# Router logits from the raw residual, rstd applied afterwards; ScalarE scales and shifts; token positions in five matmuls

## What is computed

```python
h = modulate(rmsnorm(x, norm_ffn[i]), mod[:, 3], mod[:, 4])      # h * (1 + scale) + shift
x = x + mod[:, None, 5] * moe(h, w_router, b_router, wg, wu, wd)
# moe: scores = sigmoid(h @ w_router); sel = scores + b_router
# best group of 4 experts by its two largest sel, then the top 2 inside it, weights normalised
# y = sum over the chosen experts of w_e * (silu(h @ wg_e) * (h @ wu_e)) @ wd_e
```

## Time and profile before

| | us |
|---|---|
| timed executions, median of 3 | 1325.93 (1322.24 to 1326.89) |
| span of the profiled execution | 1334.2 |
| PE busy in it | 1216.7 (91%) |
| VectorE busy | 383.0 (29%) |
| ScalarE busy | 316.9 (24%) |
| GpSimd busy | 122.9 (9%) |
| mean granted TensorE clock, of full speed | 0.956 |
| mean DMA rate | 292 GB/s |

### The profile page before, as it was taken

How to read it: one execution, slowest core, us unless ns; L and a number is a source line. 1 busy time by engine, 2 the same in 40 slices (tenths; PEclk the granted TensorE clock), 3 DMA queues, 4 the chain that set the end, 5 groups by cost and what they waited for, 6 DMA issues and landing times.

```text
span 1334.2 us, 24788 instructions
## 1 busy us (share of the span) xinstructions
PE 1216.7 (91%) x10404; PEld 720.1 (54%) x10404; DVE 383.0 (29%) x1218; ACT 316.9 (24%) x716; POOL 122.9 (9%) x188
## 2 busy tenths in 40 slices
PE   4889998889998899999979999999999987799996
PEld 2446544447885554655547643445465545575553
DVE  1345111340004422611131122341541115551113
ACT  1240111331124523211133211320311114401113
POOL 2000100210000000111120000000011120001101
PEclk9898998899999999899989999999999998889998
DMA  9999999894227874799978214882769987539993
GB/s 350 415 421 420 373 409 422 287 350 169 99 95 273 293 285 180 277 382 397 407 268 322 94 70 148 348 323 94 277 262 415 414 338 301 232 139 411 389 395 136
DMA packets 89708, 389.57 MB, mean 292 GB/s; under 512 B 10456, under 2 KB 38604, under 8 KB 53240
## 3 DMA queue, kind: packets, MB, share of 16 engines
q1 hardware_dynamic: 71568, 336.61, 65.0%
q0 software_dynamic: 17456, 51.07, 10.4%
q10 hardware_dynamic: 568, 0.23, 0.1%
HBM read 370.96 MB, written 27.96 MB: 299 GB/s over the span
## 4 chain that ended last, share of the span: by engine, by line
PE 76%; DMA 11%; DVE 5%; issue 3%; ACT 2%; POOL 1%; SPq 1%; ACTq 0%; POOLq 0%; DVEq 0%
PE bank L479 70%; DMA sb_ring<-in_w_ada 3%; PE bank L954 2%; DMA sb_ring<-in_w_exp_down 2%; DMA slot_out<-sb_arena,sb_homes 2%; DMA sb_arena<-slot_out,sb_slots 2%; DVE sb_xT L1982 1%; DMA sb_arena<-in_b_ada 1%; POOL sb_arena L2120 1%; PE bank L972 1%; DMA sb_arena<-token_rows,sb_rows 1%; DMA slot_out<-sb_arena 1%; PE bank L882 0%; DVE sb_arena L1942 0%; SPq L437 0%
## 5 line engine op out<-in xcount | busy, mean ns | idle before, releaser
L479 PE MATMUL bank<-sb_ring,sb_arena 128*32 128x256 f32 (+1 forms) x6112 | 461.8, 432 | 20.6 <-DMA sb_ring<-in_w_exp_down 7.3
L479 PEld LDWEIGHTS bank<-sb_ring,sb_arena 128*32 128x32 f32 x6112 | 232.7, 112 | 192.5 <-issue 119.7
L479 PE MATMUL bank<-sb_arena 128*128 128x128 f32 (+11 forms) x776 | 141.5, 362 | 9.3 <-DVE sb_arena L1828 5.4
L479 PE MATMUL bank<-sb_ring,sb_hT 128*128 128x256 f32 x624 | 141.4, 389 | 6.2 <-ACT sb_hT L1213 6.2
L479 PEld LDWEIGHTS bank<-sb_ring,sb_hT 128*128 128x128 f32 x624 | 121.0, 195 | 27.1 <-issue 9.1
L479 PEld LDWEIGHTS bank<-sb_arena 128*128 128x128 f32 (+2 forms) x776 | 103.6, 195 | 46.1 <-issue 13.3
L479 PE MATMUL bank<-sb_ring,sb_cond 128*2 128x512 f32 x768 | 96.8, 626 | 8.1 <-DMA sb_ring<-in_w_ada 7.7
L479 PE MATMUL bank<-sb_arena,sb_ring 128*128 128x384 f32 (+2 forms) x288 | 95.5, 507 | 3.0 <-DVE sb_arena L1698 2.1
L1929 DVE TENSOR_TENSOR sb_arena<-sb_arena,bank 128x256 f32<-128x256 f32 x40 | 16.9, 421 | 263.4 <-PE bank L479 263.4
L479 PE MATMUL bank<-sb_hT,sb_ring 128*128 128x384 f32 x256 | 84.7, 493 | 2.6 <-ACT sb_hT L1213 2.6
L479 PEld LDWEIGHTS bank<-sb_arena,sb_ring 128*128 128x128 f32 (+1 forms) x288 | 49.9, 181 | 44.9 <-issue 19.0
(11 more groups left out here) (318 smaller groups left out, 1017.8 us busy)
## 6 DMA issues: line engine op xcount, KB each, us to landing
sb_ring<-in_w_ada SPq DMA_DIRECT2D x96, 1024.0 KB, 8.3
sb_ring<-in_w_exp_gate SPq DMA_DIRECT2D x60, 1024.0 KB, 17.6
sb_ring<-in_w_exp_up SPq DMA_DIRECT2D x60, 1024.0 KB, 10.6
sb_ring<-in_w_exp_down SPq DMA_DIRECT2D x60, 1024.0 KB, 16.3
sb_ring<-in_w_mlstm_in SPq DMA_DIRECT2D x12, 1024.0 KB, 16.8
token_rows<-sb_arena POOLq DMA_DIRECT2D x12, 512.0 KB, 7.4
slot_out<-sb_arena POOLq DMA_DIRECT2D x9, 512.0 KB, 8.6
sb_scratch<-in_w_exp_gate SPq DMA_DIRECT2D x4, 1024.0 KB
```

What stands on the lines that cost most here:

```text
L479: return pe.matmul(out, lhsT, rhs, start=first, stop=last)
```

## The change

- **Logits from the residual.** VectorE multiplies `w_rt` by the two amplitude columns of the layer (`router_weights`), which gives 32 stationary columns `w_ra`: 16 for context, 16 for latent tokens. PE multiplies them with the raw residual `xT`, interleaved with the squares of the norm (`raw_logits`, `norm_routed`, bank `ps[5]`). VectorE multiplies the result by `rstd`. In layer 0 the eight raw matmuls follow the last w_ada columns instead.
- **Shift.** The product of the shift vectors with `w_rt` is computed per layer in 16 one-column matmuls (`shift_logits`): in front of the output projection in layer 1, at the start of the mixer in layers 2 and 3, behind the mixer in layer 0. Three matmuls of one row add it to the folded logits, now in `ps[4]`.
- **Normalised activations.** VectorE writes `xT * rstd` in eight instructions of 384 columns. ScalarE applies amplitude and shift in one instruction for each chunk and token kind (`modulate`), the first three chunks before the exponential of the logits, five after it.
- **Order.** The fold stands before rows 0 to 3 of the w_ada group. The transposes take the first half of the channels of all tiles first (`TURNS`). Positions take five matmuls over wider ranges. Rows 4 and 5 of the w_ada group move behind the positions, next to row 6.
- Some semaphores are merged (`turns_full`, `gate_tok`), and the arena is 96 columns smaller.

```diff
+TURNS = [0, 2, 4, 1, 3, 5]
...
+        w_ra = sb("w_ra", [P, KC, 2, NE])
...
-            def norm(n):
-                for k in range(KC):
+            def norm_squares(n, a, b):
+                for k in range(a, b):
                     if k % 2 == 0 or k == KC - 1:
                         pe.wait_ge(sq_ready, 6 * n + (k // 2 + 1 if k < KC - 1 else 5))
                     q = k % 4
                     ins = mm(ps[6][32 * q:32 * q + 32, 0:TOK], mean_ones[:, 0:32], sq[:, k, :], k < 4, k >= 4)
-                ins.then_inc(ms_full, 1)
+                if b == KC:
+                    ins.then_inc(ms_full, 1)
+
+            def norm_mean(n):
                 pe.wait_ge(sq_ready, 6 * n + 6)
                 mm(ps[6][:, 0:TOK], mean_ones[:, 32:32 + P], rstd[:, :], True, True).then_inc(ms_full, 1)
+
+            def norm(n):
+                norm_squares(n, 0, KC)
+                norm_mean(n)
+
+            def raw_logits(L, n, a, b):
+                pe.wait_ge(wra_ready, L + 1)
+                for k in range(a, b):
+                    pe.wait_ge(x_ready, 8 * n + k + 1)
+                    q = k % 4
+                    ins = mm(ps[5][32 * q:32 * q + 32, 0:TOK], w_ra[:, k, :, :].rearrange("p c e -> p (c e)"), xT[:, k, :],
+                             k < 4, k >= 4)
+                    if k >= 4:
+                        ins.then_inc(lg_full, 1)
+
+            def shift_logits(L, bank):
+                pe.wait_ge(mod_added, 3 * L + 2)
+                for c in range(2):
+                    for k in range(KC):
+                        ins = mm(bank[0:1, c * NE:(c + 1) * NE], mod[:, L, 24 + k, c:c + 1], w_rt[:, k, :], k == 0, k == KC - 1)
+                ins.then_inc(sr_full, 1)
+
+            def norm_routed(L, n):
+                if L == 0:
+                    norm(n)
+                    ada(2, 6, 7)
+                    ada_columns(2)
+                    raw_logits(L, n, 0, KC)
+                else:
+                    for a, b in ((0, 2), (2, 4), (4, 6), (6, 7), (7, 8)):
+                        raw_logits(L, n, a, b)
+                        norm_squares(n, a, b)
+                    norm_mean(n)
+                pe.wait_ge(sr_ready, L + 1)
+                for t in range(NT):
+                    c = min(t, 1)
+                    mm(ps[4][:, t * NE:(t + 1) * NE], ones[0:1, :], shift_row[:, c * NE:(c + 1) * NE], t == 0, False)
+                pe.wait_ge(lg_ready, L + 1 + (L > 0))
+                for t in range(NT):
+                    c = min(t, 1)
+                    ins = mm(ps[4][:, t * NE:(t + 1) * NE], lg[:, t * P:(t + 1) * P], fold[:, c * NE:(c + 1) * NE], False, t == NT - 1)
+                ins.then_inc(rt_full, 1)
...
+                if r:
+                    shift_logits(3, ps[7])
...
+                shift_logits(1, ps[5])
 
                 project(r, lambda k: (qT if k % 2 == 0 else kT)[:, k // 2, :], hsT_ready, [8] * KC)
...
+                shift_logits(2, ps[7])
...
             def experts(L, n):
-                side(ps[6], w_rt, n)
-                for c in range(2 * NT):
-                    if c == 2:
-                        unfold(ps[6], L + 1 + (L > 0), rt_full)
+                for c in TURNS:
+                    pe.wait_ge(h_ready, 16 * n + (8 if c % 2 == 0 else 16))
+                    if c == 4:
+                        pe.wait_ge(rt_e, L + 1)
                     for k in range(4):
                         ins = pe.transpose(ps[c][:, k * P:(k + 1) * P],
                                            hT[:, 4 * (c % 2) + k, (c // 2) * P:(c // 2 + 1) * P], ident[:, :])
                     ins.then_inc(ht_full, 1)
 
-                for g in ADA_WINDOW[L]:
-                    ada(g, 4, 5)
                 pe.wait_ge(mask_ready, L + 1)
                 pick = rt[:, 5, :]
-                for t in range(NT + 1):
-                    for q in range(min(t, NT - 1) + 1):
-                        ins = mm(ps[6][:, 64 + t * NE:64 + (t + 1) * NE], tri[:, 0:P] if q == t else ones[:, :],
-                                 pick[:, q * NE:(q + 1) * NE], q == 0, q == min(t, NT - 1))
-                ins.then_inc(pos_full, 1)
+                sums = ps[6][:, 64:64 + (NT + 1) * NE]
+                mm(sums[:, NE:], ones[:, :], pick, True, False)
+                mm(sums[:, 0:NE], tri[:, 0:P], pick[:, 0:NE], False, False)
+                mm(sums[:, NE:NT * NE], tri[:, 0:P], pick[:, NE:], False, False)
+                mm(sums[:, 2 * NE:], ones[:, :], pick[:, 0:2 * NE], False, False)
+                mm(sums[:, NT * NE:], ones[:, :], pick[:, 0:NE], False, True).then_inc(pos_full, 1)
                 for g in ADA_WINDOW[L]:
-                    ada(g, 6)
+                    ada(g, 4, 5, 6)
...
                     pe.wait_ge(const_in, 16 * NCONST)
-                if L == 0:
+                    shift_logits(0, ps[5])
                     ada(2, 0, 1, 2, 3, 4, 5)
-                norm(2 * L + 1)
-                if L == 0:
-                    ada(2, 6, 7)
-                    ada_columns(2)
+                norm_routed(L, 2 * L + 1)
...
+            def modulate(L, n, a, b):
+                gain, bias = amp[:, L, 1, :, :], mod[:, L, 24:32, :]
+                for k in range(a, b):
+                    act.wait_ge(h_scaled, 16 * n + 2 * k + 2)
+                    for c in range(2):
+                        o = h_out(k, c)
+                        act.activation(o, o, ACT.Identity, bias=bias[:, k, c:c + 1], scale=gain[:, k, c:c + 1]).then_inc(h_ready, 1)
...
+                modulate(L, n, 0, 3)
                 act.wait_ge(rt_full, L + 1)
-                act.activation(rt[:, 1, :], ps[6][:, 0:48], ACT.Exp, scale=-1.0).then_inc(rt_e, 1)
-                for c in range(2 * NT):
-                    act.wait_ge(ht_full, 2 * NT * L + c + 1)
+                act.activation(rt[:, 1, :], ps[4][:, 0:48], ACT.Exp, scale=-1.0).then_inc(rt_e, 1)
+                modulate(L, n, 3, KC)
+                for i, c in enumerate(TURNS):
+                    act.wait_ge(ht_full, 2 * NT * L + i + 1)
                     act.activation(htok[:, c // 2, :].rearrange("p (k q) -> p k q", k=KC)[:, :, (c % 2) * 64:(c % 2 + 1) * 64],
                                    ps[c][:, :].rearrange("p (q k) -> p k q", k=KC), ACT.Copy).then_inc(ht_ready, 1)
...
-                act.wait_ge(mod_added, 3 * L + 2)
-                norm_shift(2 * L + 1, mod[:, L, 24:32, :], h_out)
+                act.wait_ge(mod_added, 3 * L + 3)
...
+            def shift_copy(L, bank):
+                v.wait_ge(sr_full, L + 1)
+                v.tensor_copy(shift_row, bank[0:1, 0:2 * NE]).then_inc(sr_ready, 1)
+
+            def router_weights(L):
+                for c in range(2):
+                    ins = v.tensor_tensor(w_ra[:, :, c, :], w_rt[:, :, :], amp[:, L, 1, :, c:c + 1].to_broadcast([P, KC, NE]), ALU.mult)
+                ins.then_inc(wra_ready, 1)
+
+            def norm_routed(L, n):
+                v.wait_ge(lg_full, 4 * (L + 1 + (L > 0)))
+                v.wait_ge(rstd_ready, n + 1)
+                v.tensor_tensor(lg, ps[5][:, 0:TOK], rstd[:, :], ALU.mult).then_inc(lg_ready, 1)
+                for k in range(KC):
+                    v.tensor_tensor(hT[:, k, :], xT[:, k, :], rstd[:, :], ALU.mult).then_inc(h_scaled, 2)
...
-                copy_logits(ps[6], L + 1 + (L > 0))
...
                 norm(2 * L, amp[:, L, 0, :, :])
+                if L > 1:
+                    shift_copy(L, ps[7])
                 if kind == 0:
                     pool_mixer(2 * L)
                 elif kind == 1:
                     mlstm(2 * L)
                 else:
                     mla(2 * L)
+                if L == 1:
+                    shift_copy(L, ps[5])
+                if L:
+                    router_weights(L)
                 residual(2 * L, gpool[:, L // 3, :, :] if kind == 0 else mod[:, L, 16:24, :], lambda c: ps[c % 4], 8 * L)
                 if kind == 1:
                     mod_columns(ADA_MIXER[1][2])
                 if L == 0:
+                    shift_copy(L, ps[5])
                     mod_columns(2)
-                norm(2 * L + 1, amp[:, L, 1, :, :])
+                    router_weights(0)
+                norm_routed(L, 2 * L + 1)
...
-                    g.wait_ge(ht_ready, 2 * NT * L + 2 * t + 2)
+                    g.wait_ge(ht_ready, 2 * NT * L + NT + t + 1)
```

30 lines of the change are left out of this document (16 added, 14 removed).

## The result

The changed kernel took 1329.76 us (median of 20 executions, 1322.34 to 1335.04) beside 1325.72 us for the kernel before (20 executions, 1319.07 to 1329.23). The ratio is 1.0029, 95% interval 1.0015 to 1.0042: 0.3% slower, clear of noise but inside the half per cent that the prediction calls no change, and outside the forecast of 1318.1 (1309 to 1328). The profiled execution has a span of 1332.7 us at a mean clock of 0.950.

The account below looks back on a forecast made before the run. PE was taken as the bound (busy 91% of the span), with the weight stream binding in layer 0. Layer gains of 0.3, 1.5, 3.1 and 3.0 sum to 7.9 us off 1334.2, scaled to 1318.1 us; range 1309 to 1328.

Parts of the forecast that it names:

- the half per cent that the prediction calls no change: Whole kernel: about 6.6 us is what its measurement can tell from no change; chance of landing inside 0.38.
- e: End of the norm's mean matmul, from which stage times count; forecast 1.4, 1.1 and 1.1 us later in layers 1 to 3.
- the end of independent groups: Norm: if PE's column groups run independently, e comes 0.85 us later in layer 1, 0.5 in layers 2 and 3.
- the middle value: Norm's delay from interleaved raw-logit matmuls, taken between independent groups and program order: 1.4, 1.1, 1.1 us in layers 1 to 3.
- matmuls keep program order: Norm, rival: two column groups run at a time, e 2.1, 1.7 and 1.7 us later; 1320 us, chance 0.12.
- The step that failed: Edited stage: merged semaphores, smaller arena and new transpose order cost nothing; token copies end about e + 13.4, before the gather.
- the prediction's signs of being wrong: e moves over 2 us, ScalarE ends after e + 11, or PE's expert-weight waits grow in layers 1 to 3.
- The second failed step: w_ada ring slots: SyncE's loads released up to 4 us later, with stream slack in layer 1 (share 0.46 at 560).
- Layer 0: Stage shrinks 3 to 4 us, but the weight stream absorbs it; gain taken as 0.3 us, bounds 0 and 3.
- the forecast's 0.3, 1.5, 3.1 and 3.0: Net gains in us forecast for layers 0, 1, 2 and 3, in all 7.9 us off the profiled span.
- the gain is taken back by the weight stream: Rival, layers 1 to 3: the stream bounds the whole expert stage, absorbing gains and costs; 1326 us, chance 0.14.
- The clock rival: Fold's wait leaves PE at 1.2 GHz until the gather's end; layers 1 and 2 lose 7.5 us each; 1343, chance 0.08.

Follow-up runs that it names:

- held-back loads: Changed kernel with SyncE's weight loads, from the fifth expert unit of layers 1 and 2 on, put on hold until the token rows have landed: 1327.76 us, 1.0018.
- the path taken away: Changed kernel whose first POOL gather (tile 1, every layer) reads other rows, those of an input weight, without waiting for the token writes; wrong data: 1316.56 us, 0.9939.
- the kernel before with the same edit: Kernel before, as control, with tile 1 of every layer gathered from rows of an input weight and the overflow test held at none: 1324.85 us, 0.9996.
- the order of the transposes: Changed kernel with the transposes in the old order, tile by tile, each tile's row written out once whole: 1331.86 us, 1.0057.
- rows 4 and 5 back: Changed kernel with w_ada rows 4 and 5 put between the transposes and the positions again, row 6 staying behind the positions: 1331.26 us, 1.0038.
- ScalarE's queue: Changed kernel with the three token-row writes issued by ScalarE instead of POOL, each behind its last copy of that tile: 1326.72 us, 1.0034.
- rows 0 to 3 first: Changed kernel with the first four w_ada rows of the window put in front of the fold of the logits again: 1322.55 us, 0.9978.

## Why the prediction was wrong

**What held.** In layer 1 the selection frees PE at e + 11.1 (e + 11.2); in layers 2 and 3 the positions start at e + 12.3, when the transposes end, since w_ada rows or transposes ran at half the clock. ScalarE's 16 activations take 7.2 us, 0.90 a chunk (0.89). VectorE's eight wide products take 551 ns each while ScalarE reads, 3.83 us in all (4.2). Positions in 1.2 us, three rows behind them in 2.76 (2.7). Layer 3's gather comes at e + 17.2 (e + 16.8), layer 2's at e + 16.2. The shift's 16 matmuls are 32 passes in 0.93 us in layer 0 (1.3; bounds 0.65 and 3.9). `router_weights` 0.56 us (0.5). The norm's 16 small matmuls went in four steps of four, 2.83 us from 526.99 against 1.86 before: 1.0 us more, the end of independent groups (0.85), so the middle value was too high. The Trainium skill's rule that matmuls keep program order (TensorE: Matmul & The Clock Gate, "Part 3: Packing small matmuls") would have made it 3.8 us by the prediction's working; with 2.83 us the trace does not agree here.

**The step that failed** is the one without a price: "The fewer merged semaphores, the smaller arena and the new order of the transposes have no price: the token copies on ScalarE [...] end at about e + 13.4, behind the selection but before the gather, and GpSimd's queue sends the rows out as they come." The copies were timed rightly, and checked against the wrong consumer: PE's gather of tile 0, not POOL's write and read back for tile 1. The slack of that path could be read in the trace before: the last write went out at 537.64 and took up to 10.1 us, so the rows lay in memory by 547.7, some 5 us ahead of the row numbers at 552.95. The change brings the row numbers 5.5 us forward and the last write 0.9 us back, which eats the slack even with unchanged landings. None of the prediction's signs of being wrong watched this path: e moved by 1.0 us, ScalarE's activations ended at e + 9.7, and PE's waits for expert weights grew by 1.2 us in layers 1 to 3.

**The second failed step** is "SyncE's loads into the ring slots of these rows are released up to 4 us later; the stream then has slack in layer 1 (share 0.46 at 560)". The delay was sized rightly (4.0 us, counted from the mean's end), but it was priced by the stream's share at the wrong time and for the wrong victim: the weights weren't late, the token writes met them. In layer 1 the last landing was 16.6 us instead of 10.1, and w_ada rows 0 to 3 put first brought it back to 11.2. As an estimate, this is the whole of layer 1's wait: with a landing of 10.1 the gather would go out at 544.65 + 10.1 + 0.8 = 555.55 and bring its rows 6.25 us later, at 561.8, where PE is free at 561.7. The 6.25 us are the weak term: beside held-back loads the same gather took 9.7.

**Layer 0** was forecast as absorbed by the stream: 0.3 us gained, never a loss. The stage shrank (26.2 to 22.6 us), but a wait of PE in a stage at share 1.01 isn't free either: it stops the releases. By the profiles it costs layer 0 some 5.5 us. The times give 0.24% (1.0029 to 1.0005), about 3 us, but their intervals overlap.

**Balance.** Forecast 0.6% faster. With the path taken away the change is 0.6% faster; the path costs 0.9%; together that is 0.3% slower. That the first two agree is in part luck: the norm's term was too high, layer 0's probably too low, and what the layers gain against the kernel before with the same edit (1.8, 2.2, 6.1 and 5.7 us by the table, with the 0.7 us of raw logits counted) doesn't follow the forecast's 0.3, 1.5, 3.1 and 3.0, as far as single profiles can say. Of the rivals, "the gain is taken back by the weight stream" named the right resource and the wrong way: not waits for expert weights (19.0 us after, 17.6 before), but the stream beside another transfer. The clock rival (1343) didn't come, though half-clock spells did: the four rows behind the fold's wait took 4.88 and 6.33 us.

**What stays open.** Three edits shortened the wait, left rows 0 to 3 behind the fold and didn't gain (the order of the transposes, rows 4 and 5 back, ScalarE's queue). A part of this is that the sum of waits is a poor measure. What counts is when PE starts on the fetched rows, in us after the norm's start:

| us | layer 0 | 1 | 2 |
|---|---|---|---|
| before | 46.5 | 40.8 | 41.2 |
| changed | 46.4 | 41.4 | 41.7 |
| order of the transposes | 45.3 | 41.6 | 41.7 |
| rows 4 and 5 back | 46.0 | 39.3 | 41.9 |
| ScalarE's queue | 45.7 | 39.1 | 40.9 |
| rows 0 to 3 first | 47.6 | 37.4 | 39.3 |
| other rows | 43.2 | 38.1 | 38.2 |

The first two rows are the result in short: the gain of layers 0 to 2 is gone when PE turns to these rows. The order of the transposes moved this start by 0.9 us in all, where the waits fell by 7. For the other two, 2.3 and 3.8 us came sooner and the time still didn't fall. All three ran at mean clocks of 0.954 to 0.956; those with rows 0 to 3 first ran at 0.960 to 0.963 and were faster than the changed kernel. Over the executions of the kernel before, 0.01 of clock goes with some 7 to 10 us, so the clock would be enough to explain it, but clock and wait weren't varied apart. (The hold also left these rows behind the fold; it ran at 0.961 and gained 0.1%, at a cost of its own.) That the version with these rows first stops at 0.998, short of the 0.994 of the path taken away, is put down to layer 0's wait, which it keeps (8.6 us); that too is argued from size alone.

## What to carry to other kernels

When a chain is shortened, list every consumer that the old end released, and give each of them the slack of its own other input: here the row numbers moved forward by 5.5 us and the rows that they point to didn't. A reordering that changes when buffers are given back also moves transfers; ask which small, urgent transfer they will meet, not only whether the stream has slack later. A DMA share of 1.0 doesn't say what is in it: read the queues apart. And compare when an engine gets past a wait, not how long it waited: a wait that is reached later is shorter for nothing. Work that needs nothing (the w_ada rows) belongs in front of a wait, not behind it: that one move took the ratio from 1.0029 to 0.9978.
